# A new order of work in the second block's mixers, with inverse roots by Ln and Exp and the groups normalised one by one

## What is computed

```python
def rmsnorm(x, g):
    return x * lax.rsqrt(jnp.mean(x * x, axis=-1, keepdims=True) + EPS) * g

for l in range(DEPTH):                                   # DEPTH = 2
    xn = rmsnorm(x, norm_mix[l])
    u_pool, u_conv, u_diff, u_sc, u_mem = split(xn @ w_in[l])          # 2560 columns
    y_pool = pool_mixer(u_pool)        # windows 2..16, a 64x64 product each, scale
    y_conv = conformer_conv(u_conv)    # a * sigmoid(gate), 31 taps, layernorm, silu, 256x256
    y_diff = diff_attention(u_diff)    # q,k rms-normed by head (32), 2x4 heads, softmax each,
                                       # p0 - lam * p1, times v, rmsnorm by head (64)
    y_sc = short_conv(u_sc)            # bg * conv3(cg * h)
    y_mem = memory_attention(u_mem)    # q,k rms-normed by head (64), 4 heads over 256 memory rows
    cat = stack([y_pool, y_conv, y_diff, y_sc, y_mem])
    cat = rmsnorm(cat, group_norm[l])  # each group of 256 columns by itself
    x = x + cat @ w_out[l]             # 1280 x 1024
    x = x + peer_ffn(rmsnorm(x, norm_ffn[l]))  # 8 heads x 16 experts of 16384, gathered by token
```

## Time and profile before

| | us |
|---|---|
| median of 3 runs | 3498.9 (3497.45 to 3499.19) |
| the profiled execution | 3501.93 |
| its span | 3500.1 |
| TensorE busy in the span | 3112.3 |
| mixers, layer 0: first slab to the output matrix | 1719.7 to 1880.8 |
| mixers, layer 1 | 2607.7 to 2768.3 |

### The profile page before, as it was taken

The page is one execution under the profiler, slowest core; times in us unless marked ns, Lnnn a source line. Parts: engine busy times, 40 slices in busy tenths (PEclk is TensorE's granted clock), DMA queues, the critical chain, the costliest instruction groups (busy, mean ns, idle before and its releaser), DMA issues.

```text
span 3500.1 us, 30722 instructions
## 1 busy us (share of the span) xinstructions
PE 3112.3 (89%) x11516; PEld 2025.2 (58%) x11516; DVE 1600.6 (46%) x3728; ACT 561.2 (16%) x1431; POOL 613.0 (18%) x558
## 2 busy tenths in 40 slices
PE   9999998999999997999987887787889689777777
PEld 7858986785876897787565542222238454222222
DVE  1014324101002523310174777777755577777775
ACT  0003112100001213111122111111121311111110
POOL 0010000101001000100000344444420034444442
PEclk9999999999999999999998999999999899999999
DMA  5443322444444331354332999999973189999998
GB/s 208 167 145 129 114 83 97 145 164 148 158 155 144 132 109 61 120 217 167 108 108 79 380 420 421 421 416 413 418 297 124 61 336 378 421 421 418 413 412 357
DMA packets 114917, 830.11 MB, mean 237 GB/s; under 512 B 12880, under 2 KB 13136, under 8 KB 14160
## 3 DMA queue, kind: packets, MB, share of 16 engines
q0 software_dynamic: 73728, 536.90, 37.2%
q1 hardware_dynamic: 39456, 281.29, 23.0%
q10 hardware_dynamic: 1584, 9.95, 0.8%
HBM read 827.05 MB, written 1.05 MB: 237 GB/s over the span
## 4 chain that ended last, share of the span: by engine, by line
PE 65%; DMA 21%; DVE 8%; issue 4%; ACT 1%; POOL 0%; POOLq 0%; DVEq 0%; SPq 0%; ACTq 0%
PE bank L295 27%; DMA arena<-table_uv,idx 20%; PE bank L322 10%; PE bank L1788 8%; PE bank L1557 5%; PE bank L660 2%; PE bank L1702 2%; DVE arena L2099 1%; DVE arena L2316 1%; DVE diag L2324 1%; PE bank L1566 1%; PE bank L411 1%; DMA ring<-stream 1%; PE bank L376 1%; PE bank L515 1%
## 5 line engine op out<-in xcount | busy, mean ns | idle before, releaser
L1788 PE MATMUL bank<-arena,diag 128*128 128x512 f32 x2048 | 1003.1, 620 | 250.4 <-DVE diag L2324 249.3
L295 PE MATMUL bank<-x,ring 128*128 128x256 f32 x4256 | 934.0, 382 | 13.8 <-DMA ring<-stream 13.8
L295 PEld LDWEIGHTS bank<-x,ring 128*128 128x128 f32 x4256 | 812.2, 192 | 126.5 <-issue 10.2
L1788 PEld LDWEIGHTS bank<-arena,diag 128*128 128x128 f32 x2048 | 360.3, 191 | 876.8 <-DVE diag L2324 591.0
L2316 DVE CUSTOM_DVE_ANT_0 arena<-arena 128x1024 f32<-128x1024 f32 x512 | 625.5, 1222 | 283.1 <-DMA arena<-table_uv,idx 280.6
L2387 POOL DMA_INDIRECT arena<-table_uv,idx x512 | 543.7, 1062 | 1042.1 <-PE bank L1788 734.5
L1286 POOL TENSOR_TENSOR x_tok<-arena,ktail 128x1024 f32<-128x1024 f32 (+1 forms) x12 | 26.2, 2186 | 1672.1 <-ACT arena L685 1672.1
L322 PE MATMUL bank<-ring,hid 128*128 128x512 f32 x704 | 303.3, 592 | 0.0
L978 DVE SCALAR_TENSOR_TENSOR hid<-o_sw,bank 128x256 f32<-128x256 f32 x88 | 37.1, 421 | 567.9 <-ACT o_sw L705 567.9
L1979 ACT ACTIVATE dots<-dots 128x1 f32<-128x1 f32 x512 | 103.5, 203 | 1090.0 <-DVE dots L2316 1089.6
L322 PEld LDWEIGHTS bank<-ring,hid 128*128 128x128 f32 x704 | 133.5, 190 | 165.2 <-issue 165.0
(11 more groups left out here) (388 smaller groups left out, 2418.7 us busy)
## 6 DMA issues: line engine op xcount, KB each, us to landing
ring<-stream SPq DMA_DIRECT2D x260, 1024.0 KB, 4.8
arena<-table_uv,idx POOLq DMA_INDIRECT x512
ktail<-ln_rows ACTq DMA_DIRECT2D x6, 1024.0 KB, 6.7
arena<-mem_rows SPq DMA_DIRECT2D x2, 1024.0 KB, 10.5
sq<-keys ACTq DMA_DIRECT2D x2, 1024.0 KB, 4.7
cst<-consts SPq DMA_DIRECT2D x1, 1547.0 KB, 10.5
cst<-consts SPq DMA_DIRECT2D x1, 1089.0 KB, 14.4
x<-x_in SPq DMA_DIRECT2D x1, 1024.0 KB, 4.9
```

The lines of the kernel that those rows point to most:

```text
L295: last = mm(out[:, half * T:half * T + T], w[:, half * KC + k, :], rhs[:, k, :], start=(k == 0), stop=(k == KC - 1))
L1788: last = mm(bank[4 + 2 * tt + half][:, :], diag[:, n % DIAGS, :], rows[:, n % SLOTS, D + 512 * half:D + 512 * half + 512], start=(h == 0 a ...
```

## The change

It does six things, all in the second block.

1. The slabs have a new order: memory keys, memory values, `S_DQ, S_DK, S_GATE, S_CONV, S_UM, S_POOL, S_DV, S_H, S_BG, S_CG`. They alternate between two banks instead of three; bank 2 is used for small results.
2. TensorE, ScalarE and VectorE have a new order. The output projection of a group stands between the products of other mixers.
3. The 31 taps of the convolution are in five pieces (8, 6, 7, 7, 3) with other work between them.
4. Every inverse root is a Ln and an Exp with scale -0.5, both on ScalarE; the reciprocals on VectorE for them are gone, in the norms of rows too, and in the memory norm, which lies in the first block's last feed-forward part.
5. The five groups are squared, averaged, rooted and scaled one by one, in the order pool, difference, memory, short, convolution. The output matrix's slabs are in that order.
6. Other banks for the transposes and for the output.

The core of the diff, in the order tensor, scalar, vector, host. What is left out repeats these patterns or moves lines unchanged. `inverse_root` is used by `head_root` (four times), for the difference output, for the layernorm and by `group_inverse` (five times).

```diff
-S_MEMK, S_MEMV, S_DQ, S_DK, S_UM, S_DV, S_GATE, S_CONV, S_POOL, S_H, S_BG, S_CG = range(12)
+S_MEMK, S_MEMV, S_DQ, S_DK, S_GATE, S_CONV, S_UM, S_POOL, S_DV, S_H, S_BG, S_CG = range(12)
+MIX_BANKS = 2
+OUT_ORDER = (G_POOL, G_DIFF, G_MEM, G_SHORT, G_CONV)
+OUT_BANK = ((0, 1), (5, 6))
...
+                def group_squares(n):
+                    g = OUT_ORDER[n]
+                    pe.wait_ge(cat_sq.sem, cat_sq.at(l, n + 1))
+                    for i in range(GT):
+                        last = mm(bank[GROUP_BANK[g]][:, 0:T], c_("mean_group"), group_sq(g)[:, i * T:i * T + T],
+                                  start=(i == 0), stop=(i == GT - 1))
+                    last.then_inc(cat_ms.sem, 1)
+                project(S_DQ)
+                project(S_DK)
+                project(S_GATE)
+                head_squares(1, "mean32", 3)
+                head_squares(2, "mean32", 4)
+                head_squares(0, "mean64", 5)
+                project(S_CONV)
                 pe.wait_ge(qk_ready.sem, qk_ready.at(l, 1))
                 diff_scores(0)
-                project(S_BG)
+                project(S_UM)
                 diff_scores(4)
-                project(S_CG)
+                head_squares(3, "mean64", 7)
+                project(S_POOL)
+                project(S_DV)
+                project(S_H)
...
+                pe.wait_ge(cat_sq.sem, cat_sq.at(l, 1))
+                outputs(bank[2], dvz, dT).then_inc(do_done.sem, 1)
+                group_squares(0)
+                project(S_BG)
...
+                project(S_CG)
...
+                group_squares(1)
...
+                out_slab(0)
+                outputs(bank[3], mvz, mT).then_inc(mo_done.sem, 1)
...
+                group_squares(2)
+                pe.wait_ge(cat_std.sem, cat_std.at(l, 2))
+                group_squares(3)
+                out_slab(1)
+                group_squares(4)
                 tail = range(OUT2_SLABS - LAST, OUT2_SLABS)
...
-                fn(ss[:, tt, 1:2], ss[:, tt, 0:1], ACT.Sqrt, bias=eps[:, 0:1], scale=1.0 / D).then_inc(rms_std.sem, 1)
+                step.did(fn(ss[:, tt, 1:2], ss[:, tt, 0:1], ACT.Ln, bias=eps[:, 0:1], scale=1.0 / D))
+                step.join()
+                fn(ss[:, tt, 2:3], ss[:, tt, 1:2], ACT.Exp, scale=-0.5).then_inc(r_ready.sem, 1)
...
+                def inverse_root(dst, src, signal):
+                    step.did(fn(dst, src, ACT.Ln, bias=eps[:, 0:1]))
+                    step.join()
+                    fn(dst, dst, ACT.Exp, scale=-0.5).then_inc(signal.sem, 1)
...
+                head_root(0, 1, 3)
+                head_root(1, 2, 4)
+                head_root(2, 0, 5)
+                read(fn(sg[:, :], projected(S_GATE)[:, :], ACT.Sigmoid), S_GATE)
                 heads_with_squares(S_UM, 3, 2)
+                head_root(3, 3, 7)
...
-                fn(arena[:, 0:N_GROUPS * GT * T], cat[:, :, :].rearrange("p c t -> p (c t)"), ACT.Square).then_inc(cat_sq.sem, 1)
...
-                last = v.reciprocal(ss[:, tt, 2:3], ss[:, tt, 1:2])
-                    step.did(v.reciprocal(r, r))
-                step.did(v.reciprocal(rstd[:, :], std[:, :]))
-                step.did(v.reciprocal(sq[:, 2:4, :], sq[:, 2:4, :]))
-                    step.did(v.reciprocal(arena[:, at:at + n * T], arena[:, at:at + n * T]))
...
+                for n in range(DF_HEADS):
+                    biased(n)
+                conv_part(0, 8)
+                for n in range(DF_HEADS, 2 * DF_HEADS):
+                    biased(n)
...
+                conv_part(8, 14)
...
+                conv_part(14, 21)
...
+                conv_part(21, 28)
...
+                convolve(cv, cpad, TAPS, M_DW, range(28, TAPS)).then_inc(conv_ready.sem, 1)
...
+                group_scaled(0)
...
+                for n in range(1, N_GROUPS):
+                    group_scaled(n)
...
-        slabs[l, S_OUT:S_WQ] = rows_of(np.asarray(a["w_out_2"][l]))
+        slabs[l, S_OUT:S_WQ] = rows_of(np.asarray(a["w_out_2"][l]))[list(OUT_ORDER)]
```

More of the change, by code:

```diff
@@ L1446, in second_block @@
         memg_ready = sig("memg_ready", 1)
-        stream_free = [sig(f"stream_free{b}", len(range(b, MIX_USES, BANKS))) for b in range(BANKS)]
+        stream_free = [sig(f"stream_free{b}", len(range(b, MIX_USES, MIX_BANKS))) for b in range(MIX_BANKS)]
         qk_sq = sig("qk_sq", 4)
@@ L1591, in tensor, with head_squares @@
                     xn_waits(l, 0, tt)
-                for u in (S_DQ, S_DK, S_UM, S_DV):
-                    project(u)
-                for i, m in enumerate(("mean64", "mean32", "mean32", "mean64")):
+                def head_squares(i, m, b):
                     pe.wait_ge(qk_sq.sem, qk_sq.at(l, i + 1))
-                    mm(bank[3 + i][:, :], c_(m), sq[:, 2 * i:2 * i + 2, :].rearrange("p c t -> p (c t)"),
+                    mm(bank[b][:, :], c_(m), sq[:, 2 * i:2 * i + 2, :].rearrange("p c t -> p (c t)"),
                        start=True, stop=True).then_inc(qk_ms.sem, 1)
-                for u in (S_GATE, S_CONV, S_POOL, S_H):
-                    project(u)
                 def diff_scores(first):
@@ L1801, in mem_scalar @@
                 for tt in range(TT):
-                    fn(ss[:, tt, 1:2], ss[:, tt, 0:1], ACT.Sqrt, bias=eps[:, 0:1], scale=1.0 / D).then_inc(mem_std, 1)
+                    step.did(fn(ss[:, tt, 1:2], ss[:, tt, 0:1], ACT.Ln, bias=eps[:, 0:1], scale=1.0 / D))
+                step.join()
+                for tt in range(TT):
+                    fn(ss[:, tt, 2:3], ss[:, tt, 1:2], ACT.Exp, scale=-0.5).then_inc(mem_std, 1)
             if j == MEM2_T_AT:
@@ L1899, in scalar @@
                        accum_out=sm[:, 2, n:n + 1]).then_inc(ds_exp.sem, 1)
+                values(S_DV, dvz)
+                read(fn(sh[:, :, :].rearrange("p a t -> p (a t)"), projected(S_H)[:, :], ACT.Copy), S_H)
+                for h in range(DF_HEADS):
+                    act.wait_ge(dt_done.sem, dt_done.at(l, h + 1))
+                    fn(dT[:, 4 * h:4 * h + 4, :].rearrange("p b q -> p (b q)"), bank[3 + h][:, :],
+                       ACT.Copy).then_inc(dt_copied.sem, 1)
+                act.wait_ge(poolw_done.sem, poolw_done.at(l, 1))
+                for i in range(GT):
+                    scale = prm[:, M_PSCALE + i:M_PSCALE + i + 1]
+                    fn(cat[:, i, :], bank[2][:, i * T:i * T + T], ACT.Copy, scale=scale)
+                    last = fn(group_sq(G_POOL)[:, i * T:i * T + T], bank[2][:, i * T:i * T + T], ACT.Square, scale=scale)
+                last.then_inc(cat_sq.sem, 1)
                 for h in range(MA_HEADS):
@@ L2102, in convolve, with biased @@
                     return last
-                dve.wait_ge(stream_free[S_CONV % BANKS].sem, stream_free[S_CONV % BANKS].at(l, S_CONV // BANKS + 1))
-                step.did(convolve(cv, cpad, TAPS, M_DW, range(FIRST_TAPS)))
-                for n in range(8):
+                def biased(n):
                     h = n % DF_HEADS
@@ L2113, in vector, with conv_part @@
                         cst[:, at:at + TT * T], ALU.mult, ALU.add).then_inc(ds_biased.sem, 1)
+                def conv_part(first, end):
+                    step.did(convolve(cv, cpad, TAPS, M_DW, range(first, end)))
+                for n in range(DF_HEADS):
+                    biased(n)
+                dve.wait_ge(stream_free[S_CONV % MIX_BANKS].sem, stream_free[S_CONV % MIX_BANKS].at(l, S_CONV // MIX_BANKS + 1))
+                conv_part(0, 8)
+                for n in range(DF_HEADS, 2 * DF_HEADS):
+                    biased(n)
                 dve.wait_ge(ds_biased.sem, ds_biased.at(l, 8))
```

307 lines of the change are left out of this document (144 added, 163 removed).

## The result

The changed kernel takes 3435.9 us (3435.31 to 3438.64, four runs) where the kernel before takes 3498.6: a ratio of 0.982, 95% interval 0.981 to 0.984. I had said 3430, and 69.0 us of gain; it is 62.7.

| stretch | before | after | change | predicted |
|---|---|---|---|---|
| span start to `S_MEMK`, layer 0 (first block) | 1719.71 | 1717.36 | -2.35 | 0 |
| `S_MEMK` to `S_DQ`, layer 0 | 15.77 | 17.83 | +2.06 | +1.8 |
| `S_DQ` to first query, layer 0 | 180.64 | 146.80 | -33.84 | -38.0 |
| first query to the second half's transposes, layer 0 | 3.98 | 6.57 | +2.59 | +2.6 |
| from there to `S_MEMK`, layer 1 (gathers) | 687.6 | 687.5 | -0.1 | 0 |

A forecast was written before the change was run, and what follows sets the result against it. The mixers were taken as bound by a chain of dependencies, not one busy engine. 2 x (38.0 - 2.6) - 1.8 = 69.0 us off the median 3498.9 gives 3429.9, stated as 3430; range 3412 to 3450.

The forecast's parts named there:

- Tables: On ScalarE, each Ln and each Exp needs its own table load of 1.28 us; 24 loads a layer in the mixers.
- one-set rival: One table set serves Ln and Exp: 5 loads in the mixers instead of 24, norms lose nothing, 3419 us; chance 12%.
- The first gap: TensorE idles 1.9 us before the first scores, waiting for the third head root on ScalarE after S_CONV ends.
- The second gap: TensorE idles 1.8 us before the transposes, waiting for the softmax difference, in place of 18.2.
- contention factor: In the hand-laid schedule, VectorE's instructions beside GpSimd's pooling were lengthened 1.6 times.
- Low clock: In the mixers, TensorE's granted clock was to be near 1.00 all through, so no time was added for it.
- thin-covers rival: Margins of 0.4 to 2.3 us fail, low clock follows longer gaps: 10 to 20 us a layer less, 3442 to 3475; 13%.
- no 0.5 in the windows: Sign to check in the profile's windows: granted clock near 1.00 all through, never 0.5.
- Covers: After the second wait no TensorE wait lasts in the mixers; five margins of 0.4 to 2.3 us hide the other engines' work.
- The norms: Row norm after the output: two loads, Ln and Exp add 2.6 us a layer; start of layer 0 adds 1.8 us.
- Slower, or nothing: Two rivals: another engine bounds the mixers, no gain, 2%; ScalarE's queue becomes the bound, near 3535 with 4 us loads, 3%.
- longer gathers: Sign that the prediction is wrong: the gathers behind the mixers take longer than before; their predicted change was 0.

The follow-up runs named there:

- one_set: The changed kernel with the table set holding both Ln and Exp loaded by name at four places, so neither needs its own load; 3426.3 us.
- unspread: The changed kernel with the first two output slabs moved from between the small products to behind the last group's mean of squares; 3469.8 us.
- norm_by_sqrt: The changed kernel with Sqrt and reciprocal back in the second block's row norms only, the mixers keeping Ln and Exp; 3426.1 us.
- two_pieces: The changed kernel with the convolution in two pieces (taps 0 to 15 and 16 to 30) instead of five; 3445.3 us.
- no_pooling: The changed kernel without GpSimd's sliding sums, so that the pool mixer gives zero; 3433.7 us.
- four_taps: one_set with the convolution's second piece cut to taps 8 to 11 from 8 to 13, the next piece starting at tap 12; 3422.9 us.
- mean_bank2: The changed kernel with the memory keys' mean of squares in bank 2 instead of 5, so the first scores don't wait for the third head root; 3434.9 us.
- early_exp: four_taps with ScalarE's copy of S_POOL behind the fifth exponential instead of ahead of the first, and the middle piece taps 8 to 10; 3419.3 us.

## Why the prediction was right, and by how much not

- *The bound.* Mixers made of dependencies, TensorE's own work 138.5 us. Right: both layers add up to 138.5, the listed gaps and the low clock to within 0.1 us.
- *Tables.* A load before each Ln and each Exp of the roots, with the sigmoid's and the Silu's 24 a layer: right, as is 1.28 us for each and 3.9 for a root pair. The one-set rival did not come by itself, but is to be had by name, and I had priced it at 11 us below the forecast, and `one_set` is 9.6 to 12.3 below the changed kernel.
- *The first gap.* 1.9 predicted, 2.07 measured, by the cause named.
- *The second gap.* 1.8 predicted, 2.71 measured. The term mis-sized is the contention factor, 1.6 in the layout, for which the prediction shows no row; for the taps it is 2.1 (0.85 for 0.40). The twelve instructions end 1.7 us behind the last exponential. I had them end together. 2 x 0.9 us.
- *Low clock.* The step that failed. I had granted full clock "all through" in the forecast, and low clock only in the thin-covers rival, "behind longer gaps". Gaps of 2.07 and 2.71 us were long enough: three times 1.76 us in the profiled execution, 5.3 us, the largest part of the miss. The sign that I had named, no 0.5 in the windows, was not met: layer 0 has a granted 0.50 at its first scores. By the earlier trace rows I had only gaps of 3.05 and more with low clock behind them, and should have kept both ends for the shorter ones. One row I also misread: the first scores there take 6.25 us behind a gap of 4.17, and I put 2.8 of them down to waits. The granted clock is 0.50 in the first 2.4 us of them and 0.65 in the next 4, with TensorE busy throughout, so nearly all of it was low clock.
- *The sum of these.* 2 x 0.17 + 2 x 0.9 + 5.3 = 7.4 us more in the mixers than 2 x 142.2, and 291.9 - 284.4 = 7.5 is what the table has. That the total missed by less, 5.7 us between the profiled spans, is luck: the first block, which the change leaves alone, was 2.35 us shorter.
- *Covers.* None of the five was paid: the convolution's last tap ended at 2680.8 for a mean at 2682.4, and no wait is listed behind the transposes. `unspread` shows that the cover was needed. The thin-covers rival is out, though low clock, which it had and the forecast had not, came behind the two gaps.
- *The norms.* +2.6 a layer predicted and +2.6 measured; the start of layer 0 +1.8 and +2.06, with gaps of 1.49 and 0.40 where I had 1.4 and 0.6.
- *Slower, or nothing.* ScalarE is busy 77.6 of 145 us from `S_DQ` to the first query, 33 more than before (I had 32 more), and no bound. VectorE loses 26.8 us there; the 18.5 of the prediction left out the reciprocals of the groups.

Two things of the time are not settled. The gathers of layer 1 took 1.0 us longer; the query behind the 2.83 us gap there takes 4.87 us, at low clock, where it takes 3.84 behind the same gap in layer 0. In the changed kernel run again layer 1 too has the gap with 3.84 behind it, and its gathers take 691.6 us, 0.9 less than before. So the sign that I had named, longer gathers, is not met by every execution, and the low clock is 1.0 us of the 1.9 between the two. And why one gap of 2.07 us is followed by low clock and another isn't stays open (below).

## To carry over

Read what ends each long wait before pricing any operation: the new order was worth 58 of 63 us, while taking 27 us of VectorE's work out of each layer of the old order gave 4 by the medians and 6 to 7 in its trace, since the largest wait ended through other work. A function that needs another table costs nothing under cover and 1.28 us a load at the end of a chain, so ask for a set that holds both functions by name where a chain ends in them, or keep the old form there. What stands ahead of a late result in an in-order list matters more than its own cost: one copy moved by five places, with one tap, took 1.3 and 2.1 us off a gap.

## What the hardware showed beyond that

- **Low clock after a gap of 2 us.** TensorE at a granted 0.50 (the 1.2 GHz level) in the 2.5 us behind a 2.07 us gap (layer 0), 0.63 and 0.73 in layer 1, and 1.00 behind the same gap in `norm_by_sqrt`. Of twelve gaps of 2.07 us before the scores in the six kernels that have it (the changed kernel and again, `norm_by_sqrt`, `unspread`, `two_pieces`, `no_pooling`), nine had low clock behind them. Of the fifteen gaps of 2.6 to 2.9 us before the transposes, in the kernels with such a gap, ten had it. Behind the two of 2.15 in `two_pieces`, the one of 1.77 in `four_taps` and the four of 1.05 to 1.13 us (`mean_bank2`, `no_pooling`) there was none. The loss behind a gap of 2.07 is 1.8 us in each of the nine cases, nearly the gap once more. The length of the gap alone does not decide it.

```profile
1768.00:1770.50 2.50, 2.50 (x8) 1.96 (x7) 1.00 (x2) 1.38 (x2) 0.00 (x0) 0.50 0.70 295
...
2615.90:2619.60 3.70, 3.70 (x17) 3.29 (x18) 1.85 (x4) 1.73 (x2) 0.00 (x0) 1.00 0.58 241
```

The first row is a window of the changed kernel, the second of `norm_by_sqrt`, each right behind its gap (columns as above).

- **VectorE beside GpSimd.** SCALAR_TENSOR_TENSOR on 256 columns 0.40 alone and 0.85 beside the pooling, on 512 columns 0.75 and 1.3 to 1.4, TENSOR_SCALAR on 256 columns 0.29 and 0.78 (1.14 and 3.11 us for four); RECIPROCAL on 512 columns 3.35 and 3.34. It goes the other way too: GpSimd's first addition took 3.43 us instead of 1.1 in layer 0 of `four_taps`, and in `early_exp` its four products took 5.33 instead of 3.33 while the softmax's TENSOR_TENSOR ran beside them at its 2.29.
